# Tap sizes in PSUM, the causal block added per head, GpSimd's sums in turns, and memory values made with tokens on partitions

## The chip, the core and the metric

The kernel runs on one core of a Trainium2 chip: TensorE (PE), VectorE (DVE), ScalarE (ACT), GpSimd (POOL) and SyncE (SP, which here only issues transfers). The metric is the device time of one execution in microseconds (us).

## The reference, cut to what matters

Two transformer-like blocks over 512 tokens of width 1024, in float32. The first block mixes with four kinds of heads (a short convolution, a dilated attention, a forgetting attention, a pooling mixer), then attends to a memory of 256 tokens, then runs a convolutional feed-forward part. The second block is a long convolution (Hyena) with a filter made by a small network, then a gated feed-forward part. What the change touches:

```python
# forgetting attention, 4 heads, query block i of 128 tokens
s = einsum("bhqd,bhkd->bhqk", qi * scale, k) + ci[..., None] - c[:, :, None, :]
s = where(kpos[None, :] <= t[:, None], s, NEG_INF);  p = softmax(s);  out = p @ v
# memory attention
k, v = split(memn @ w_kv, 2)          # 256 tokens x 1024, 4 heads of 256
# filter of the long convolution: taps, and their size per channel
h = (h @ w_out).reshape(L, 2, D) * exp(-t[:, :, None] * abs(decay))
g = concatenate([h[:, 0], 0, flip(h[1:, 1])]);  g = g / sum(abs(g), axis=0)
# gates of the forgetting attention: log_sigmoid(x_n @ w_gate + b), summed over tokens
```

## The kernel before, in words

The code writes out by hand what each engine does and in which order; engines run their own list in order and wait on named semaphores. The order within a list is therefore fixed, and a wait holds up all that stands behind it on that engine.

Weights come in pairs of 1 MB (`raw`, two buffers). ACT makes the high part of each pair (`w_hi`, L501), DVE the low part (`w_lo`, L931, signal `lo_ready`), and PE multiplies with three passes (high by high L1577, and the two mixed products L1578 and L1579), which stands in for a float32 product. A chunk is half a pair.

**The first 100 us**: `in_chunk(c)` makes the projections of the first block, 24 matmuls each. Between them PE runs small jobs in two spare banks: the norm's sum, the gates (64 matmuls with 4 output columns, L1714, and 4 with one, L1716), three layers of the filter's network (`mlp`, L1683), four rotations for the rotary embedding (`rotate`, L1689). DVE answers in a written order (`mlp_args`, `rope_cos`, `rope_sin_part`), ACT too.

**The unit loop**: `for u in range(32)`, one unit per head and query block; the heads with u of 16 or more are the forgetting attention. In each iteration PE makes the scores of unit u + 2 (`qk_unit`, L1766), one chunk of weights, the transposes of unit u - 1 (L1775) and the product with the values of unit u - 2 (L1785). DVE adds the bias and takes the minimum (`mask_unit`, L1128 and L1136, signal `masked`), normalises (L1142) and splits weights; ACT exponentiates (L618) and makes the bias (L628). With i = u - 16, iterations 16 to 31 carry two more jobs:

- `mem_chunk(i)`: chunks 0 to 7 make the memory's keys, 8 to 15 its values. Before, the values come out with features on partitions, DVE scales them into `v_stage` (L1246), PE transposes them (`mem_values`, L1842) into bank 2, and DVE copies them to `v_mem` (L1251).
- for every second i, `filter_taps(t)`, t = i/2: PE makes taps into banks 2 and 3 (L1823), DVE multiplies them by a decay that ACT made (L1214 and L650), ACT takes their sizes (`tap_sizes`, L673) into two tiles of SBUF, DVE adds those to `acc` (L1226, signal `size_sum`). POOL forms sums and differences of the taps (`gen`, L430 and L431) and folds them (L437); after the last fold it issues two small loads (L441) that ACT copies into the matrix `g_fwd` (L731, signal `g_patched`).

Behind the loop PE sums the sizes (`filter_size`, L1832), transforms the filter in eight steps (`filter_spectrum`, L1908), and goes on to `w_out` and the rest of the kernel, which the change leaves as it is.

Of the kernel before, what the change touches and what calls it, by code (L numbers as in the profile page):

```python
# [18 lines left out]
ALU = mybir.AluOpType  # L19
# [59 lines left out]
JOBS = ["norm", "gates", "mlp0", "norm_mem", "mlp1", "rot0", "rot1", "rot2", "rot3", "mlp2", "vt0", "vt1", "c_tok", "c_row",  # L79
# [17 lines left out]
def program(nc, a):  # L97
    with ExitStack() as ctx:
# [5 lines left out]
        def sem(name):  # L104
# [31 lines left out]
        rstd_tok = at("rstd_tok", [P, 4], F32, o); o += 32  # L136
        log_f = at("log_f", [P, 4, 4], F32, o); o += 64
# [47 lines left out]
        v_stage = at("v_stage", [P, 2, M], F32, 12 * KB)  # L185
# [5 lines left out]
        c_keys = [at("c_keys0", [P, T], F32, c2 + 6 * KB), at("c_keys1", [P, T], F32, 14 * KB)]  # L191
        bias = at("bias", [P, T], F32, c2 + 8 * KB)
# [6 lines left out]
        size_taps = [at("size_taps0", [P, T], F32, 58 * KB), at("size_taps1", [P, T], F32, 74 * KB)]  # L199
# [30 lines left out]
        tri_in, pool_in, late_in, mask_in, diag_in, x_again = (sem(n) for n in (  # L230
            "tri_in", "pool_in", "late_in", "mask_in", "diag_in", "x_again"))
# [23 lines left out]
        vt_done, vt_read = sem("vt_done"), sem("vt_read")  # L255
# [57 lines left out]


# [57 lines left out]
        def _(pool):  # L372
# [24 lines left out]
            def load_filter(half):  # L397

                cols = slice(half * T, (half + 1) * T)
                for rows in (slice(0, 64), slice(64, P)):  # L400
                    pool.dma_start(f_out[rows], a["f_out"][:, :, cols]).then_inc(late_in, 16)
                pool.dma_start(decay[:], a["decay"][:, :, cols]).then_inc(late_in, 16)

# [8 lines left out]
            load_filter(0)  # L412

            for t in range(8):
                half, n, w = t // 4, t // 2 % 2, t % 2
                eo = eo_gen[half]
                if t in (2, 4):

                    pool.wait_ge(biased, 2 * t)
                    load_keys(1 + t // 2)  # L420
                if t == 3:

                    pool.wait_ge(gen_exp, 8)
                    pool.wait_ge(gen_done, 4)
                    load_filter(1)
                pool.wait_ge(gen_taps, 2 * t + 2)
                if w == 0 and t:
                    pool.wait_ge(gen_fold, 2 * t)
# [3 lines left out]
                if w:  # L432
                    pool.wait_ge(gen_sum, 2 * t + 2)
                    pool.wait_ge(tap_size, 2 * t + 2)
                    z, d, x, y = (gen[:, i, :] for i in range(4))
                    for kind, one, other, op in ((0, z, x, ALU.add), (1, d, y, ALU.subtract), (2, d, y, ALU.add), (3, z, x, ALU.subtract)):
                        nc.gpsimd.tensor_tensor(eo[:, 2 * kind + n, :], one, other, op).then_inc(gen_fold, 1)  # L437
# [11 lines left out]
            pool.wait_ge(vt_done, 4)  # L449
# [40 lines left out]
        def _(act):  # L490
# [94 lines left out]
            root(1, M)  # L585
# [6 lines left out]
            A.activation(gate_tmp[:, 2, :], gate_tmp[:, 1, :], ACT.Ln, bias=1.0).then_inc(gate_log, 1)  # L592
            v_copy(5)
            mlp_layer(1)
            raw_copy(2)
            raw_copy(3)
# [24 lines left out]
            def bias_unit(u):  # L621

                s, i = UNITS[u]
                if i == 0:
                    act.wait_ge(c_keys_in[s % 2], 16 * ((s - 4) // 2 + 1))
                if u > 16:
                    act.wait_ge(masked, u)
                A.activation(bias[:, 0:(i + 1) * P], c_keys[s % 2][:, 0:(i + 1) * P], ACT.Identity,  # L628
                             bias=c_neg[:, i, s - 4:s - 3]).then_inc(biased, 1)
# [13 lines left out]
            def decays(t):  # L643

                half, n, w = t // 4, t // 2 % 2, t % 2
                act.wait_ge(decay_abs, half + 1)
# [6 lines left out]
            def keep_token0(half):  # L653

                act.wait_ge(token0_done, half + 1)
                if half:
                    act.wait_ge(biased, 12)
                    act.wait_ge(size_sum, 16)
                else:
                    act.wait_ge(masked, 16)  # L660
                A.copy(g_token0[half][:], ps[:, 3, :]).then_inc(token0_kept, 1)
                A.activation(size_taps[0][0:1, :], ps[0:1, 3, :], ACT.Abs).then_inc(token0_kept, 1)

            def tap_sizes(t):

                half, n, w = t // 4, t // 2 % 2, t % 2
                if t:
                    act.wait_ge(size_sum, 2 * t)
                else:
                    act.wait_ge(token0_size, 1)  # L670
                for d in range(2):
                    act.wait_ge(gen_taps, 2 * t + d + 1)
                    A.activation(size_taps[d][:], eo_gen[half][:, 4 * w + 2 * d + n, :], ACT.Abs).then_inc(tap_size, 1)  # L673

            exp_unit(0)
            for u in range(32):
# [36 lines left out]
                if i >= 0 and i % 2 == 1:  # L713
                    tap_sizes(i // 2)
                if i == 14:
                    act.wait_ge(qk_done, 32)
                    for q in range(2):
                        src = a["weights"][G_DRAM + q].rearrange("p (j r n c) -> p j r n c", j=2, r=2, n=4)
                        dst = g_fwd[:, q * CHUNK:(q + 1) * CHUNK].rearrange("p (j r n c) -> p j r n c", j=2, r=2, n=2)
                        for r in range(2):  # L720
                            act.dma_start(dst[:, :, r], src[:, :, r, 0:2, :]).then_inc(g_fwd_in, 16)
            keep_token0(1)
            copy_transposed(31, T)
            act.wait_ge(token0_size, 2)
            out_tile(5)
# [3 lines left out]
            for q in range(2):  # L729
                rows = g_fwd[0:1, q * CHUNK:(q + 1) * CHUNK].rearrange("p (j r n c) -> p j r n c", j=2, r=2, n=2)  # L730
                A.copy(rows[:, :, q, 0, :], mid_row_g[:, 2 * q:2 * q + 2, :]).then_inc(g_patched, 1)  # L731
                if q:
                    for j in range(2):
                        A.activation(rows[:, j, 0, 0, :], ones[0:1, :], ACT.Copy, scale=0.0).then_inc(g_patched, 1)
            split_pair(19)
# [188 lines left out]
        def _(dve):  # L924
# [134 lines left out]
            V.tensor_scalar(mean[:, 0:M], bank[:, 0:M], 1.0 / D, EPS, ALU.mult, ALU.add).then_inc(norm_mean, 1)  # L1059
            dve.wait_ge(norm_mean, 2)  # L1060
            V.engine_nop().then_inc(read, 1)
            dve.wait_ge(norm_root, 2)
            V.reciprocal(rstd_mem[:], mean[:, 0:M]).then_inc(norm_rstd, 1)
# [28 lines left out]
            rope_cos(1)  # L1092
            split_pair(4)
# [3 lines left out]
            rope_sin_part(0)  # L1097
            rope_sin_part(1)
# [1153 lines left out]
```

## Time and profile before

| what | us |
|---|---|
| median of three executions | 1525.85 (1521.45 to 1526.17) |
| the profiled execution, device time | 1526.68 |
| its span in the profile | 1524.8 |
| PE busy | 1459.8 (96%) |
| DVE busy | 883.6 (58%) |
| ACT busy | 552.8 (36%) |
| POOL busy | 120.1 (8%) |

In rows of the profile, a row of the timeline is: start, duration, engine, line, operation, output <- inputs, shapes, count, and in brackets the idle time just before it with what ended it. "PEclk" is the granted clock of TensorE as a share of 2.4 GHz; 0.50 is 1.2 GHz.

### The profile page before, as it was taken

Reading aid. Unit: us, or ns where it says so; the run is one execution under the profiler, and the core shown is the slowest. Engines: PE = TensorE matmul, PEld = TensorE weight load, DVE = VectorE, ACT = ScalarE, POOL = GpSimd, SP = SyncE. Lnnn points to the kernel's source line nnn. Section 1 sums busy time; section 2 is a strip of 40 time slices with the busy share of each in tenths; the row PEclk is TensorE's granted clock in tenths of the full one; section 3 lists DMA queues with packets and bytes.
Section 4 is the critical chain, followed back from the end, with each engine's and each line's share of the span. In section 5 each row is a group of like instructions: output and inputs, shape, how many; then the busy total and the mean of one; then the engine's idle time right before and its main releaser. Section 6 shows DMA issues by size and latency. Waiting matters only on the chain.

```text
span 1524.8 us, 17410 instructions
## 1 busy us (share of the span) xinstructions
PE 1459.8 (96%) x6492; PEld 1163.5 (76%) x6492; DVE 883.6 (58%) x1152; ACT 552.8 (36%) x736; POOL 120.1 (8%) x134
## 2 busy tenths in 40 slices
PE   7899998889998999999999999999999999999995
PEld 6776667646886888888888878886788888888884
DVE  6745588633543577547736687675775433443446
ACT  5424355322333354324323454441233322221231
POOL 1000043420000000000000022103100000000000
PEclk9799997889998999999999999999999999999998
DMA  6211222332220223232323233223122222222221
GB/s 243 75 56 56 97 91 90 109 140 83 83 83 29 83 83 110 84 110 83 110 83 111 83 111 110 83 97 138 42 87 107 86 99 96 105 88 106 90 104 56
DMA packets 25501, 144.01 MB, mean 94 GB/s; under 512 B 3058, under 2 KB 6283, under 8 KB 10720
## 3 DMA queue, kind: packets, MB, share of 16 engines
q1 hardware_dynamic: 20464, 127.93, 23.8%
q0 software_dynamic: 3168, 11.87, 2.2%
q10 hardware_dynamic: 1808, 3.35, 0.6%
q8 instruction: 43, 0.70, 0.2%
q14 instruction: 18, 0.15, 0.0%
HBM read 136.84 MB, written 6.30 MB: 94 GB/s over the span
## 4 chain that ended last, share of the span: by engine, by line
PE 88%; DVE 6%; ACT 3%; issue 2%; DMA 1%; POOL 0%; DVEq 0%; SPq 0%; ACTq 0%; POOLq 0%
PE ps L1577 26%; PE ps L1579 25%; PE ps L1578 25%; PE ps L1908 2%; ACT w_hi L501 1%; DVE w_lo L931 1%; DVE acc L1226 1%; PE ps L1963 1%; PE ps L1785 1%; PE ps L1766 1%; PE ps L1950 1%; PE ps L1714 1%; PE ps L1823 1%; PE ps L2073 1%; PE ps L1775 1%
## 5 line engine op out<-in xcount | busy, mean ns | idle before, releaser
L1577 PE MATMUL ps<-opA_hi,w_hi 128*128 128x512 f32 x1120 | 445.8, 398 | 10.1 <-DVE opA_lo L976 9.5
L1579 PE MATMUL ps<-opA_hi,w_lo 128*128 128x512 f32 x1120 | 438.6, 392 | 0.0
L1578 PE MATMUL ps<-opA_lo,w_hi 128*128 128x512 f32 x1120 | 438.5, 392 | 0.0
L931 DVE TENSOR_TENSOR w_lo<-raw,w_hi 128x2048 fp32r<-128x2048 f32 x114 | 263.9, 2315 | 125.9 <-ACT w_hi L501 124.0
L501 ACT CAST w_hi<-raw 128x2048 fp32r<-128x2048 f32 x113 | 215.4, 1907 | 328.7 <-PE ps L1579 328.6
L1577 PEld LDWEIGHTS ps<-opA_hi,w_hi 128*128 128x128 f32 x1120 | 212.0, 189 | 63.6 <-issue 19.3
L1578 PEld LDWEIGHTS ps<-opA_lo,w_hi 128*128 128x128 f32 x1120 | 211.9, 189 | 45.1 <-issue 1.7
L1579 PEld LDWEIGHTS ps<-opA_hi,w_lo 128*128 128x128 f32 x1120 | 211.7, 189 | 45.0
L1577 PE MATMUL ps<-opB_hi,w_hi 128*128 128x512 f32 x576 | 227.6, 395 | 7.1 <-DVE spec L1502 2.8
L1579 PE MATMUL ps<-opB_hi,w_lo 128*128 128x512 f32 x576 | 225.8, 392 | 0.0
L1578 PE MATMUL ps<-opB_lo,w_hi 128*128 128x512 f32 x576 | 225.7, 392 | 0.0
L1577 PEld LDWEIGHTS ps<-opB_hi,w_hi 128*128 128x128 f32 x576 | 109.0, 189 | 35.1 <-issue 8.1
L1579 PEld LDWEIGHTS ps<-opB_hi,w_lo 128*128 128x128 f32 x576 | 109.0, 189 | 22.9
L1578 PEld LDWEIGHTS ps<-opB_lo,w_hi 128*128 128x128 f32 x576 | 109.1, 189 | 22.3
L1548 DVE TENSOR_TENSOR z_pad<-ps,rstd 128x512 f32<-128x512 f32 x44 | 30.1, 687 | 79.1 <-PE ps L1579 78.9
L1426 DVE TENSOR_TENSOR h<-ps,h 128x512 f32 x32 | 22.1, 691 | 81.5 <-PE ps L1579 81.5
L1403 DVE SCALAR_TENSOR_TENSOR conv<-z_pad,vecs,conv 128x512 f32<-128x512 f32 x88 | 64.0, 748 | 6.4 <-DVE conv L1403 0.5
L811 ACT CAST opB_hi<-conv 128x512 f32 x44 | 27.3, 620 | 107.6 <-DVE conv L1552 67.3
L967 DVE TENSOR_TENSOR opB_lo<-conv,opB_hi 128x512 f32 x44 | 30.5, 693 | 40.1 <-ACT opB_hi L811 40.1
L1336 DVE TENSOR_TENSOR h<-ps,h 128x512 f32<-128x512 f32 x32 | 22.1, 691 | 43.4 <-PE ps L1579 42.7
L753 ACT ACTIVATE opA_hi<-h,vecs 128x512 fp32r<-128x512 f32 x24 | 17.3, 723 | 76.5 <-DVE h L1336 51.9
L463 POOL TENSOR_TENSOR acc_next<-acc_next,sq_next 128x512 f32<-128x512 f32 x8 | 11.2, 1399 | 407.0 <-ACT sq_next L758 407.0
(326 smaller groups left out, 1544.8 us busy)
## 6 DMA issues: line engine op xcount, KB each, us to landing
raw<-weights_dram SPq DMA_DIRECT2D x113, 1024.0 KB, 4.8
g_dram<-g_stage POOLq DMA_DIRECT2D x8, 512.0 KB, 2.9
h<-x_t_dram SPq DMA_DIRECT2D x4, 512.0 KB, 8.1
h<-x_t_dram POOLq DMA_DIRECT2D x1, 2048.0 KB, 8.4
scores<-g_dram SPq DMA_DIRECT2D x4, 512.0 KB, 4.1
g_spec<-g_dram SPq DMA_DIRECT2D x4, 512.0 KB, 3.3
out_dram<-h ACTq DMA_DIRECT2D x4, 512.0 KB, 2.7
raw<-weights_dram SPq DMA_DIRECT2D x2, 512.0 KB, 6.6
```

What stands on the lines that cost most here:

```text
L501: A.copy(w_hi[:, p, :], raw[:, p, :]).then_inc(hi_ready, 1)
L811: A.copy(op_hi[1][:, bass.ds(2 * i + p, 1), :].rearrange("p a t -> p (a t)"), conv[:, p, 0, :] if not gated_only else conv[:, p, 1, :]).th ...
L931: V.tensor_tensor(w_lo[:, p, :], raw[:, p, :], w_hi[:, p, :].bitcast(F32), ALU.subtract).then_inc(lo_ready, 1)
L967: return V.tensor_tensor(out, src, hi.bitcast(F32), ALU.subtract)
L1336: V.tensor_tensor(h[:, k, :], ps[:, c % 4, :], h[:, k, :], ALU.add).then_inc(bank_read, 1)
L1403: ins = V.scalar_tensor_tensor(conv[:, p, j, :], z_pad[:, p, j, tap:tap + T], vecs[:, bass.ds(2 * i + (VEC["ffconv"] + tap * 2 * FT + j * ...
L1426: V.tensor_tensor(hd, ps[:, 2 * p + j, :], hd, ALU.add).then_inc(bank_read, 1)
L1548: V.tensor_tensor(z_pad[:, p, j, 0:T], ps[:, 2 * p + j, :], rstd[:], ALU.mult).then_inc(bank_read, 1)
L1577: W.matmul(out, w[0], x[0], start=start, stop=False, skip_group_check=mixed)
L1578: W.matmul(out, w[0], x[1], start=False, stop=False, skip_group_check=mixed)
L1579: return W.matmul(out, w[1], x[0], start=False, stop=stop, skip_group_check=mixed)
L1908: last = W.matmul(ps[:, bank + r, :], g_fwd[:, at_w:at_w + P], eo_gen[half][:, 2 * kind + k, :], start=(k == 0), stop=(k == 1))
```

## The change

Nine edits, all before 355 us of the profiled execution:

1. **Tap sizes in PSUM**: ACT writes them over the raw taps in banks 2 and 3, DVE adds them from there, in the same (odd) iteration; PE's next taps wait for that sum (`size_sum`) instead of for the product.
2. **Causal block per head**: POOL adds the 128 x 128 causal block to all four diagonal blocks of a head's keys at once (`diagonal_keys`); ACT makes the diagonal part of a unit's bias from it, in an instruction of its own. DVE's addition is gone.
3. **POOL in turns**: the sums of tap t start only when the split with `lo_ready` 13 + t is done, and half of each fold moves to the next turn.
4. **Memory values with tokens on partitions**: in chunks 8 to 15 the memory is the stationary operand and both halves of a weight pair move, 128 tokens by 256 features; DVE scales by a value per partition into `v_mem`. The transposes, `v_stage` and the copies are gone; `norm_mem` makes two columns more.
5. The absolute value of `decay` goes from DVE to ACT; the second load of `f_out` and `decay` goes from POOL's queue to ACT's, after `tap_sizes(3)`.
6. `filter_size(1)` comes after the second spectrum step, in bank 6; `token0_product(1)` uses bank 4.
7. ACT patches `g_fwd` before `out_tile(5)`.
8. `w_out` may start when seven of eight spectrum steps are read.
9. In the first stage the gates' four groups stand between quarters of `in_chunk(3)`, and `mlp(1)` behind `in_chunk(6)`, with the rotations ahead of it on PE, DVE and ACT.

```diff
+            def diagonal_keys(head):
+                pool.wait_ge(c_keys_in[head % 2], 16 * (head // 2 + 1))
+                nc.gpsimd.tensor_tensor(c_diag[head % 2][:].rearrange("p (i t) -> p i t", i=NT),
+                                        c_keys[head % 2][:].rearrange("p (i t) -> p i t", i=NT),
+                                        diag[:].unsqueeze(1).to_broadcast([P, NT, P]), ALU.add).then_inc(c_diag_made[head % 2], 1)
...
             for t in range(8):
-                if t in (2, 4):
-                    pool.wait_ge(biased, 2 * t)
-                    load_keys(1 + t // 2)
-                if t == 3:
-                    pool.wait_ge(gen_exp, 8)
-                    pool.wait_ge(gen_done, 4)
-                    load_filter(1)
+                if t < 7:
+                    pool.wait_ge(lo_ready, 13 + t)
+                if t in (0, 2):
+                    pool.wait_ge(biased, 4 + 2 * t)
+                    load_keys(2 + t // 2)
+                if w == 0 and t:
+                    fold(t - 1, (2, 3))
+                    pool.wait_ge(gen_fold, 2 * t)
                 pool.wait_ge(gen_taps, 2 * t + 2)
...
                 if w:
                     pool.wait_ge(gen_sum, 2 * t + 2)
                     pool.wait_ge(tap_size, 2 * t + 2)
+                    fold(t, (0, 1))
+                if t in (1, 3):
+                    diagonal_keys(2 + t // 2)
+            fold(7, (2, 3))
...
             def tap_sizes(t):
-                if t:
-                    act.wait_ge(size_sum, 2 * t)
                 for d in range(2):
                     act.wait_ge(gen_taps, 2 * t + d + 1)
-                    A.activation(size_taps[d][:], eo_gen[half][:, 4 * w + 2 * d + n, :], ACT.Abs).then_inc(tap_size, 1)
+                    A.activation(ps[:, 2 + d, :], eo_gen[half][:, 4 * w + 2 * d + n, :], ACT.Abs).then_inc(tap_size, 1)
...
+                if i == 7:
+                    act.wait_ge(gen_done, 4)
+                    act.wait_ge(gen_exp, 8)
+                    load_filter(act, 1)
...
-                    V.tensor_tensor(acc[:], acc[:], size_taps[d][:], ALU.add).then_inc(size_sum, 1)
+                    V.tensor_tensor(acc[:], acc[:], ps[:, 2 + d, :], ALU.add).then_inc(size_sum, 1)
...
-                V.tensor_tensor(dst, ps[:, i % 2, 0:M], rstd_mem[:], ALU.mult).then_inc(m_read, 1)
+                if i < 8:
+                    V.tensor_tensor(k_mem[:, i, :], ps[:, i % 2, 0:M], rstd_mem[:], ALU.mult).then_inc(m_read, 1)
+                else:
+                    hd, b = (i - 8) // 2, i % 2
+                    V.tensor_scalar(v_mem[:, b, hd * M:(hd + 1) * M], ps[:, b, 0:M], rstd_mem_tok[:, b:b + 1], None,
+                                    ALU.mult).then_inc(m_read, 1)
...
-                if i >= 2 and i % 2 == 0:
-                    add_sizes(i // 2 - 1)
+                if i >= 0 and i % 2 == 1:
+                    add_sizes(i // 2)
...
             def filter_taps(t):
-                    pe.wait_ge(gen_taps, 2 * t)
+                    pe.wait_ge(size_sum, 2 * t)
                 if t == 4:
-                    pe.wait_ge(late_in, 96)
-                if t >= 5:
-                    pe.wait_ge(vt_read, t - 4)
+                    pe.wait_ge(late_in[1], 48)
```

What moves is shown as the engines' lists have it; numbers behind a name tell buffers of one name apart.

PE, in the first stage: `in_chunk(3)` (L1577 to L1579 before), then the gates. Before:

```order
L1579 MATMUL ps<-opA_hi,w_lo 128x512
L1714 MATMUL ps<-gate_w,h 128x4 [waits gate_folded]
L1714 MATMUL ps<-gate_w,h 128x4 x7
L1716 MATMUL ps<-ones,acc 128x1
L1714 MATMUL ps<-gate_w,h 128x4 x8
L1716 MATMUL ps<-ones,acc 128x1
```

and of the change:

```order
L1729 MATMUL ps<-gate_w,h 128x4 x7
L1731 MATMUL ps<-ones,acc 128x1
L1591 MATMUL ps<-opA_hi,w_hi 128x512
L1592 MATMUL ps<-opA_lo,w_hi 128x512
L1593 MATMUL ps<-opA_hi,w_lo 128x512
L1591 MATMUL ps<-opA_hi,w_hi 128x512
L1592 MATMUL ps<-opA_lo,w_hi 128x512
L1593 MATMUL ps<-opA_hi,w_lo 128x512
L1729 MATMUL ps<-gate_w,h 128x4 x8
```

Six full matmuls now stand between two groups of small ones.

POOL, the sums and folds of taps 1 and 2 (L430, L431 and L437 before). Before:

```order
L430 TENSOR_TENSOR gen<-eo_gen_132 128x512 [waits gen_taps]
L431 TENSOR_TENSOR gen<-eo_gen_132 128x512
L437 TENSOR_TENSOR eo_gen_132<-gen 128x512 [waits tap_size,gen_sum]
L437 TENSOR_TENSOR eo_gen_132<-gen 128x512 x3
L395 DMA c_keys_126<-c_dram 128x512 [waits biased]
L430 TENSOR_TENSOR gen<-eo_gen_132 128x512 [waits gen_fold,gen_taps]
L431 TENSOR_TENSOR gen<-eo_gen_132 128x512
```

and of the change:

```order
L450 TENSOR_TENSOR gen<-eo_gen_134 128x512 [waits gen_taps,lo_ready]
L451 TENSOR_TENSOR gen<-eo_gen_134 128x512
L433 TENSOR_TENSOR eo_gen_134<-gen 128x512 [waits tap_size,gen_sum]
L433 TENSOR_TENSOR eo_gen_134<-gen 128x512
L419 TENSOR_TENSOR c_diag_128<-c_keys_126,diag 128x512 [waits c_keys_in0]
L404 DMA c_keys_127<-c_dram 128x512 [waits biased,lo_ready]
L433 TENSOR_TENSOR eo_gen_134<-gen 128x512 x2
L450 TENSOR_TENSOR gen<-eo_gen_134 128x512 [waits gen_taps,gen_fold]
L451 TENSOR_TENSOR gen<-eo_gen_134 128x512
```

Each turn now holds at most five operations and waits for a weight split; two folds of four come a turn later, and the causal block is new.

ACT, around the second load of the filter's matrix and decay, in iterations 23 and 24 of the change (before, POOL issued them and DVE took the absolute value):

```order
L697 ACTIVATE ps<-eo_gen_134 128x512 [waits gen_taps] x2
L321 DMA f_out<-f_out_dram 64x2x512 [waits gen_exp,gen_done]
L321 DMA f_out<-f_out_dram 64x2x512
L322 DMA decay<-decay_dram 128x2x512
L522 CAST w_hi<-raw 128x2048 [waits chunk_done,raw_in1]
L639 ACTIVATE scores,total<-scores,low 128x256 [waits masked]
L651 ACTIVATE bias<-c_keys_126,c_neg 128x256 [waits masked]
L652 ACTIVATE bias<-c_diag_128,c_neg 128x128
L660 COPY probs_t<-ps 128x512 [waits pv_done,transposed]
L672 ACTIVATE decay<-decay 128x1024 [waits late_in1]
L677 ACTIVATE eo_gen_135<-decay,vecs 128x512 [waits decay_abs]
```

The loads are issued one iteration ahead of the instruction that waits for them.

## Rows read from the trace of the kernel before

**Rows 1.** The page: TensorE's clock in 40 slices of the span.

```profile
PEclk9799997889998999999999999999999999999998
```

**Rows 2.** Stretches: busy time and count of each engine, clock, DMA share, GB/s.

```profile
38.40:52.10 13.70, 13.70 (x55) 11.96 (x55) 11.36 (x24) 5.05 (x8) 2.12 (x4) 0.50 0.37 130
60.30:72.50 12.20, 8.34 (x22) 4.84 (x21) 9.38 (x17) 8.82 (x12) 0.00 (x0) 0.72 0.25 86
197.47:221.00 23.53, 22.57 (x146) 17.20 (x144) 19.98 (x35) 14.67 (x28) 10.54 (x7) 1.00 0.18 64
221.00:300.76 79.76, 66.12 (x371) 53.00 (x370) 60.88 (x94) 34.71 (x65) 33.44 (x25) 0.85 0.31 97
300.76:319.32 18.56, 12.67 (x64) 10.48 (x64) 10.62 (x13) 5.33 (x12) 10.70 (x9) 0.70 0.32 107
```

**Rows 3.** PE's waits, 196 to 320 us: total, times, longest.

```profile
PE ps L1766 <- DVE low L1136: 7.0, 4, 2.8
PE ps L1823 <- DVE v_mem L1251: 4.6, 2, 2.4
PE ps L1832 <- DVE acc L1219: 3.5, 1, 3.5
PE ps L1908 <- DVE filter_norm L1237: 2.4, 1, 2.4
PE ps L1832 <- DVE acc L1226: 1.9, 1, 1.9
```

**Rows 4.** DVE's groups, 221.00 to 300.76 us: busy, mean ns, idle before.

```profile
L931 DVE TENSOR_TENSOR w_lo<-raw,w_hi 128x2048 fp32r<-128x2048 f32 x6 | 16.2, 2702 | 7.0 <-ACT w_hi L501 7.0
L1226 DVE TENSOR_TENSOR acc<-acc,size_taps 128x512 f32<-128x512 f32 x10 | 15.8, 1577 | 0.2
L1128 DVE TENSOR_TENSOR bias<-bias,diag 128x128 f32<-128x128 f32 x10 | 6.8, 685 | 1.4 <-ACT bias L628 1.2
L1214 DVE TENSOR_TENSOR eo_gen<-ps,eo_gen 128x512 f32<-128x512 f32 x10 | 6.4, 681 | 5.3 <-PE ps L1823 5.3
L1232 DVE SCALAR_TENSOR_TENSOR decay<-decay 128x1024 f32<-128x1024 f32 x1 | 2.3, 2302 | 1.6 <-DMA decay<-decay_dram 1.6
L1251 DVE COPY v_mem<-ps 128x512 f32<-128x512 f32 x3 | 2.0, 679 | 0.0
```

**Rows 5.** Timeline of DVE and POOL, 198 to 226 us.

```profile
198.87 0.28 DVE L1128 TENSOR_TENSOR bias<-bias,diag 128x128 f32<-128x128 f32 x1
206.19 2.29 DVE L931 TENSOR_TENSOR w_lo<-raw,w_hi 128x2048 fp32r<-128x2048 f32 x1 [0.36 <-ACT w_hi L501]
224.01 1.27 POOL L430 TENSOR_TENSOR gen<-eo_gen 128x512 f32<-128x512 f32 x1
```

**Rows 6.** Timeline of PE: chunks 1 and 5, and unit 22's scores.

```profile
198.42 0.39 PE L1577 MATMUL ps<-mg_hi,w_hi 128*128 128x256 f32 x1
213.96 0.91 PE L1766 MATMUL ps<-qk 64*128 64x384 f32 x2 [0.95 <-DVE low L1136]
221.00 0.39 PE L1577 MATMUL ps<-mg_hi,w_hi 128*128 128x256 f32 x1
```

**Rows 7.** The last taps and what follows, by engine.

```profile
300.86 1.29 DVE L1214 TENSOR_TENSOR eo_gen<-ps,eo_gen 128x512 f32<-128x512 f32 x2 [1.80 <-PE ps L1823]
307.42 5.82 POOL L437 TENSOR_TENSOR eo_gen<-gen 128x512 f32<-128x512 f32 x4 [1.84 <-ACT size_taps L673]
313.19 1.04 POOL L441 DMA_DIRECT2D mid_row_g<-weights_dram  x2
354.95 0.47 PE L1577 MATMUL ps<-opB_hi,w_hi 128*128 128x512 f32 x1 [1.01 <-DVEq L1322]
```

**Rows 8.** The tile `decay`, 150 to 360 us: its loads' time to landing.

```profile
DMA to landing us min/median/max: 4.9/6.0/7.0
```

**Rows 9.** First stage, PE: the third gates group, and a rotation.

```profile
38.78 3.55 PE L1714 MATMUL ps<-gate_w,h 128*128 128x4 f32 x16
66.91 2.07 PE L1689 MATMUL ps<-rope_raw,rot 128*128 128x512 f32 x2 [3.25 <-DVE mlp_x L1042]
```

More of the change, by code:

```diff
@@ L312, in end, with load_filter @@
                 self.origin, self.n = None, self.before + count * self.per
+        def load_filter(queue, half):
+            cols = slice(half * T, (half + 1) * T)
+            for rows in (slice(0, 64), slice(64, P)):
+                queue.dma_start(f_out[rows], a["f_out"][:, :, cols]).then_inc(late_in[half], 16)
+            queue.dma_start(decay[:], a["decay"][:, :, cols]).then_inc(late_in[half], 16)
         @block.sync
@@ L411, in _, with fold @@
             pool.wait_ge(sc_mul, 2)
-            load_filter(0)
+            load_filter(pool, 0)
+            def diagonal_keys(head):
[3 more added lines that the diff above has]
+                                        diag[:].unsqueeze(1).to_broadcast([P, NT, P]), ALU.add).then_inc(c_diag_made[head % 2], 1)
+            pool.wait_ge(diag_in, 16)
+            diagonal_keys(0)
+            diagonal_keys(1)
+            def fold(t, kinds):
+                half, n = t // 4, t // 2 % 2
+                z, d, x, y = (gen[:, i, :] for i in range(4))
+                for kind in kinds:
+                    one, other, op = ((z, x, ALU.add), (d, y, ALU.subtract), (d, y, ALU.add), (z, x, ALU.subtract))[kind]
+                    nc.gpsimd.tensor_tensor(eo_gen[half][:, 2 * kind + n, :], one, other, op).then_inc(gen_fold, 1)
             for t in range(8):
@@ L645, in decays @@
                 half, n, w = t // 4, t // 2 % 2, t % 2
+                if t % 4 == 0:
+                    act.wait_ge(late_in[half], 48)
+                    A.activation(decay[:], decay[:], ACT.Abs).then_inc(decay_abs, 1)
                 act.wait_ge(decay_abs, half + 1)
@@ L734, in _ @@
                         A.activation(rows[:, j, 0, 0, :], ones[0:1, :], ACT.Copy, scale=0.0).then_inc(g_patched, 1)
+            act.wait_ge(biased, 16)
+            out_tile(5)
             split_pair(19)
@@ L1058, in _ @@
             bank, read = job_bank("norm_mem")
-            V.tensor_scalar(mean[:, 0:M], bank[:, 0:M], 1.0 / D, EPS, ALU.mult, ALU.add).then_inc(norm_mean, 1)
+            V.tensor_scalar(mean[:, 0:M + 2], bank[:, 0:M + 2], 1.0 / D, EPS, ALU.mult, ALU.add).then_inc(norm_mean, 1)
             dve.wait_ge(norm_mean, 2)
@@ L1721, in _ @@
             pe.wait_ge(mem_sum, 5)
-            W.matmul(out[:, 0:M], ones[:], acc[:, 0:M], start=True, stop=True).then_inc(misc_done, 1)
+            W.matmul(out[:, 0:M], ones[:], acc[:, 0:M], start=True, stop=True)
+            for b in range(2):
+                last = W.matmul(out[:, M + b:M + b + 1], acc[:, b * P:(b + 1) * P], ones[:, 0:1], start=True, stop=True)
+            last.then_inc(misc_done, 1)
             in_chunk(5)
-            mlp(1)
             rotate(0)
@@ L1727, in _ @@
             in_chunk(6)
+            mlp(1)
             rotate(2)
             rotate(3)
+            in_chunk(7)
             mlp(2)
-            in_chunk(7)
             transpose_v(0, 0)
```

138 lines of the change are left out of this document (58 added, 80 removed).

## The prediction, made before the changed kernel ran

> **What bounds the kernel now.** I read the page first: TensorE's clock stands at 9 tenths or more in most of the 40 slices and dips in two places, slices 2 and 3 and slices 7 to 9 (38 us each) [rows 1]. Behind 355 us the clock is full to the end and the change touches nothing there, so whatever it is worth lies in the first 355 us. Next the stretches [rows 2]. Each shows which of two things costs PE its time: busy short of the stretch means PE waits, a clock under 1.00 means that it works at 1.2 GHz for a part. From 38.40 to 52.10 PE is busy throughout at clock 0.50. From 60.30 to 72.50 it is busy for 8.34 of 12.20 us at 0.72. From 197.47 to 221.00 all is well: 22.57 of 23.53 us at 1.00. From 221.00 to 300.76 it is busy for 66.12 of 79.76 us at 0.85, and from 300.76 to 319.32 for 12.67 of 18.56 at 0.70.
>
> The waits name the causes in the unit loop [rows 3]: 7.0 us for `masked` (DVE late with a unit's bias and minimum), 4.6 us for the copy of the memory values out of bank 2, 1.9, 3.5 and 2.4 us for the sums of tap sizes and what follows. All but one end on DVE, which is busy for only 60.88 of 79.76 us, but in a written order. Its groups say why [rows 4]. The addition of tap sizes, 128 x 512, takes 1577 ns, while the product of the same shape that reads one operand from PSUM takes 681. The 128 x 128 addition of the causal block takes 0.28 us alone [rows 5] and 685 ns in the mean here. A weight split takes 2.29 us alone [rows 5] and 2702 ns here. Those three read both operands from SBUF and slow down while POOL works (a POOL operation takes 1.27 us [rows 5]); the product beside them does not.
>
> **The unit loop: the main term.** What PE needs without waits is read from chunks 1 and 5: 221.00 - 198.42 = 22.58 us, less the one wait of 0.95, is 21.63 for four units, 5.41 each [rows 6]. From chunk 5 to chunk 15 are ten units, 54.1 us, and about 1 us more for the sum of sizes inside it. Against 79.76 [rows 2] that leaves 24.7, and with the wait of 0.95 ahead of it 25.6 us to be had if nothing else binds.
>
> Does DVE fit into 55 us? Taken from its 60.9: the size additions become one-operand-from-PSUM, 15.8 - 10 x 0.68 = 9.0; the block additions 6.8; the splits' excess 16.2 - 6 x 2.29 = 2.5; the absolute value 2.3; the copies of values 2.0 [rows 4, 5]. That leaves 38.3 of 55. ACT has 34.7 [rows 2]; a second bias instruction in three of four units and the absolute value (2.3 us on DVE, which I keep as the bound) bring it to some 41. POOL has 33.4 us of work, less what it spends blocked; a turn is four or five operations of 1.27 us, 5 to 6.4 us, and a period of two units is 10.8, so a turn that starts behind one split is over before the next. The values' chunks keep their 24 matmuls of 256 columns, so PE pays nothing for them and loses the transposes.
>
> The new wait: PE's taps now wait for `size_sum`. Behind it on PE stand the next unit's scores and chunk. The chain is ACT's copy, two absolute values and two additions, at some 0.7 us each (nearest row: 681 ns) and partly side by side, about 2.5 us behind the transposes of the odd unit; PE has one unit, about 5 us, before it asks. Cost nothing; if that cover were gone, a late sum would cost its lateness seven times.
>
> The load on ACT's queue is what I charge. `load_filter(act, 1)` stands behind `tap_sizes(3)`, about 1.5 us behind the transposes of unit 22, and PE asks for it 5 us behind those. Three issues and a landing of 4.9 to 7.0 us [rows 8] make it 1 to 4.5 us late. I take 2.8, plus 1 us for the clock, since the waits of 2.3 to 2.8 us before were each followed by a stretch at 1.2 GHz. Zero to 7.5 are the bounds. What is late next is ACT's own absolute value and decays, and DVE's product behind them, some 2 us, inside DVE's reserve.
>
> Unit loop: 25.6 - 3.8 = 21.8 us (18 to 25.6).
>
> **The end of the loop.** From chunk 15 to the first spectrum step were 18.56 us [rows 2]. DVE's last product ends at 302.15, POOL's folds at 313.24, its two loads are issued by 314.23 [rows 7]. In the change PE no longer waits for the sum of sizes, but for POOL's queue. Measured from chunk 15: the last split is done some 1.4 us ahead of it; turn 6 (two folds, two sums) ends at 3.7, the sums of tap 7 at 6.2, four folds at 11.3. From the last fold to a patched matrix there were at most 6.1 us before, with `out_tile` and PE's own waits in it; I take 3.6. So PE starts at 14.9 instead of 18.56: 3.7 us (1 to 5). PE sits idle for some 7 of them.
>
> **Spectrum and `w_out`.** `filter_size(1)` adds about 1.0 between two steps. `w_out` no longer waits 1.01 us [rows 7]. Together nothing.
>
> **The first stage.** The stretch at 1.2 GHz from 38.40 lasts 13.70 us, in which half the speed is lost: 6.9 us [rows 2]. It begins in the gates' groups, whose third takes 3.55 us [rows 9], and PE was never idle ahead of it. The stretch from 60.30 holds 3.86 us of waiting (3.25 of them ahead of a rotation, for DVE's read of `mlp(1)`'s bank [rows 9]) and, with the clock at 1.2 GHz for 6.8 us of which some 1.2 are idle, 2.8 us of lost speed. The new order puts both rotations and `in_chunk(6)` ahead of `mlp(1)`, so that wait has a chunk's cover: 3.9 + 2.8 = 6.7 us. The interleaved gates are the open cost: nothing, if the clock falls once as before; up to 6.9 more if it holds, of which PE gives some 3 back, since DVE's chain to `norm_mem` and `rope_cos(0)` keeps its length; 3 us less if the clock falls earlier and stays down through all four groups. I take "falls once", 6.7 (3.5 to 10.6), since between small groups of 1.8 us (half of 3.55, which is at 1.2 GHz) only six full matmuls stand.
>
> The Trainium skill speaks to it in "TensorE: Matmul & The Clock Gate", section "What's actually happening": the slow clock is the default and activity releases it. By that rule more full work inside the stretch is all to the good; this trace agrees so far that PE was busy with 4-column matmuls when the clock fell, not idle. It would make 1490 of the sum below.
>
> **Sum.** 21.8 + 3.7 + 0 + 6.7 = 32.2 us off the profiled 1526.7 (span 1524.8, about 1.9 around it), which stands 0.8 above the median: 1494.5, and I say 1494.
>
> **Rivals.**
> - *Clock holds through the gates* (0.2): 3.9 more, 1490. For it: six full matmuls between groups. Against: six of them take less time than the small group beside them.
> - *DVE or ACT binds the loop* (0.15): the order of `mask_unit`, split, taps and sizes leaves an idle engine and a late `masked`. If each period of two units takes 12.3 instead of 10.8 us, 7 us of the gain go, and the slow clock after each wait costs as much again: 1508. For it: ACT's idle time today all ends on DVE. Against: 38 of 55 us.
> - *POOL still collides* (0.1): the turns only set the earliest start, and `normalise` falls into them. Ten of them behind a POOL operation of 1.27 us would add 12.7 us to DVE's 38.3; that fills 51 of 55 and costs some 5 us: 1500. Against: the splits, the largest, stand outside the turns. The Trainium skill, "SBUF — State Buffer", section "SBUF: two separate sides", has it that DVE and GpSimd take one shared port pair in turns, each for a whole instruction, and that instructions in a two-port mode count too, not only those with two SBUF inputs. The rows agree with it for two inputs (0.28 against 685 ns).
> - *Slower than before* (0.04): PE waits for `size_sum` in every period. It decides from a chain of 10 us behind the transposes instead of 2.5: seven waits of 5 us are 35, more than all the gains, 1530. Nothing in the rows asks for it.
> - *No change* (0.03): the end of the loop eats the rest, because POOL's chain, now tied to the splits, ends 28 us later than I put it. It would need POOL operations of over 4 us.
>
> **Chances.** My forecast with its own range of 1488 to 1501 has 0.48. The range that leaves out no more than 2 in 10 adds the clock that holds, POOL's collisions and part of the loop's rival: 1484 to 1509. A difference of under 0.3% (4.6 us) can't be told from none in this kernel. Faster 0.93, the same 0.03, slower 0.04.
>
> **What would show it.** In the changed profile: DVE's size additions near 0.69 us; PE's waits for `masked` and `v_mem` gone, one wait of 1 to 4.5 us ahead of the fifth taps; ten units in about 58 us; PE idle for 6 to 8 us ahead of the first spectrum step, released by ACT's patch; a stretch at 1.2 GHz still beginning between 35 and 42 us; no wait of 3 us at the rotations. The prediction is wrong if the taps wait for `size_sum`, or if the scores still wait for DVE.

## The result, and the profile after

The changed kernel takes 1487.45 us in the median of four runs (1486.48 to 1490.03) against 1524.91 of the kernel before: a ratio of 0.9762, 95% interval 0.9737 to 0.9786. I had said 1494, with a range of 1484 to 1509. The profiled execution has a span of 1485.3 us, 39.5 less than the 1524.8 before; the sum in the prediction was 32.2. So 7.3 us more than in my sum are to be found.

The page's row of TensorE's clock, to be read beside [rows 1]:

```profile
PEclk9999999899999999999999999999999999999998
```

The first dip of before, which I had left where it was, is gone; of the second one slice is left, from 260 to 297 us, around the wait ahead of the first spectrum step. The stretches of the changed kernel, with the columns of [rows 2]: the gates' four groups with the quarters between them, chunks 1 to 5, chunks 5 to 15, chunk 15 to the first spectrum step, the spectrum to the first matmul of `w_out`:

```profile
30.54:42.78 12.24, 12.24 (x93) 11.46 (x93) 11.52 (x17) 1.98 (x2) 0.00 (x0) 1.00 0.18 75
187.25:208.79 21.54, 21.54 (x143) 17.00 (x142) 17.89 (x33) 15.73 (x31) 4.87 (x5) 1.00 0.20 68
208.79:267.07 58.28, 55.65 (x358) 44.17 (x357) 40.72 (x78) 37.81 (x73) 27.69 (x23) 0.97 0.33 115
267.07:283.12 16.05, 7.46 (x53) 5.86 (x52) 5.33 (x8) 4.26 (x11) 13.79 (x13) 0.81 0.47 143
283.12:317.23 34.11, 34.11 (x81) 14.09 (x81) 9.03 (x12) 6.26 (x9) 3.75 (x7) 0.94 0.45 182
```

Where the 39.5 us came from is read by the start of the same matmul in both traces. The first matmul of `c_tok` moved from 90.38 to 79.31 (11.1 us; I had said 6.7), and chunk 1 keeps that distance within 0.1. Chunks 1 to 15 give 1.0 and 21.5 (79.76 to 58.28), together 22.5 (said: 21.8). From chunk 15 to the spectrum 18.56 became 16.05: 2.5 (said: 3.7). The spectrum up to `w_out` gives 1.5 (said: 0), and everything behind it another 1.8 (said: 0): 11.1 + 0.1 + 22.5 + 2.5 + 1.5 + 1.8 = 39.5. Against the sum's terms that is 4.4 + 0.1 + 0.7 - 1.2 + 1.5 + 1.8 = 7.3: the first stage is where I was wrong.

PE's waits in the first 330 us, longest first, to be read beside [rows 3]. The first stands at the kernel's start and is there in both traces:

```profile
PE ps L1591 <- DVE opA_lo L1004: 9.6, 1, 9.6
PE ps L1922 <- issue: 8.6, 1, 8.6
PE ps L1828 <- DVE filter_norm L1259: 1.6, 1, 1.6
PE ps L1850 <- DMA decay<-decay_dram: 1.1, 1, 1.1
```

And DVE's groups in chunks 5 to 15, beside [rows 4]:

```profile
L959 DVE TENSOR_TENSOR w_lo<-raw,w_hi 128x2048 fp32r<-128x2048 f32 x5 | 11.4, 2289 | 0.8 <-ACT w_hi L522 0.8
L1252 DVE TENSOR_TENSOR acc<-acc,ps 128x512 f32<-128x512 f32 x10 | 6.9, 687 | 2.9 <-ACT ps L697 2.7
```

The size addition takes 687 ns instead of 1577, the split 2289 instead of 2702, and DVE is busy for 40.72 of 58.28 us. Of all the waits for DVE in the ten units one is left: 1.6 us for `filter_norm`, which I had overlooked. PE's one long wait now stands ahead of the first spectrum step, where the trace names no releaser ("issue"). The timelines of POOL, ACT and PE around it name one:

```profile
266.39 2.53 POOL L433 TENSOR_TENSOR eo_gen<-gen 128x512 f32<-128x512 f32 x2 [5.57 <-DVE w_lo L959]
269.00 1.35 POOL L450 TENSOR_TENSOR gen<-eo_gen 128x512 f32<-128x512 f32 x1
...
274.12 5.37 POOL L433 TENSOR_TENSOR eo_gen<-gen 128x512 f32<-128x512 f32 x4
279.44 1.03 POOL L462 DMA_DIRECT2D mid_row_g<-weights_dram  x2
...
281.90 0.71 ACT L757 COPY g_fwd<-mid_row_g 1x256 f32<-1x256 f32 x2 [7.56 <-DMA mid_row_g<-weights_dram]
...
283.12 5.74 PE L1922 MATMUL ps<-eo_gen,g_fwd 128*128 128x512 f32 x8 [8.59 <-issue]
```

The last turn waits for a split (5.57 us), POOL works its queue off, then issues two loads of 1 KB, and ACT sits idle for 7.56 us until they land.

### The profile page after: what moved, and what is told of

Its sections match the earlier page's. It is cut to its first block, busy times and chain, and to the rows that moved or that the text cites. A ratio compares the mean times of both kernels' runs of the same rounds, so it can differ in the third digit from the quotient of the medians.

```text
span 1485.3 us, 17372 instructions
## 1 busy us (share of the span) xinstructions
PE 1432.9 (96%) x6480; PEld 1143.4 (77%) x6480; DVE 856.3 (58%) x1131; ACT 558.7 (38%) x750; POOL 115.5 (8%) x135
## 4 chain that ended last, share of the span: by engine, by line
PE 91%; DVE 5%; ACT 2%; issue 1%; DMA 1%; ACTq 0%; DVEq 0%; SPq 0%
PE ps L1591 26%; PE ps L1593 25%; PE ps L1592 25%; PE ps L1922 2%; PE ps L1803 1%; PE ps L1784 1%; PE ps L1978 1%; PE ps L1850 1%; DVE w_lo L959 1%; PE ps L1965 1%; PE ps L1793 1%; ACT w_hi L522 1%; PE ps L1828 1%; PE ps L2088 1%; PE ps L1829 0%
```

## Experiments

Eleven kernels ran. Ratios are to the kernel before in the same set of runs. Its median was 1524.91 us in the changed kernel's set and 1524.65, 1522.96 and 1522.37 in those of the experiments, and its single executions lie up to 10.3 us apart. So medians of different sets that differ by 2 or 3 us say nothing by themselves, and I go by the start of the same matmul in the traces, of which there is one for each kernel. "Up to `w_out`" is the part that the change touches; what lies behind it is taken up at the end. Edits 5 to 8 were not run alone. None of these kernels leaves out or changes any part of what is computed.

**1. The two small loads ahead of the folds.**

```diff
+                if t == 4:
+                    pool.wait_ge(s_read, 4)
+                    (the two loads of mid_row_g)
...
             fold(7, (2, 3))
-            pool.wait_ge(s_read, 4)
-            (the two loads of mid_row_g)
```

> The changed kernel with one move: GpSimd issues its two small loads of mid_row_g at the start of turn 4 instead of behind the last fold. Theory (the idle time of 8.59 us ahead of the first spectrum step is the place of these two loads in GpSimd's queue, and nothing else): the first four steps read only the first half of the folds, which were done near 246 us, so TensorE starts once ScalarE has patched g_fwd, near 276 us of the profile instead of 283.12, with 1.5 us idle; the loop's stretch at 1.2 GHz of 10.24 us (5.1 us of lost speed) shrinks or goes. Sum: 7 to 12 us under the changed kernel, 1476 to 1480 us. Rival (the folds themselves bind, as my prediction reckoned when it counted them one by one): the wait only moves to the fifth step, which needs the last fold, or to the store of the first step's result, which is queued on GpSimd behind the folds; then 0 to 3 us, 1484 to 1487.

Measured: 1477.38 us (1475.38 to 1480.58), ratio 0.9705 (0.9667 to 0.9743), 10 us under the changed kernel. Its timeline, ACT and PE, and then the stretch from chunk 15 to the first step:

```profile
275.45 0.71 ACT L758 COPY g_fwd<-mid_row_g 1x256 f32<-1x256 f32 x2 [1.12 <-DMA g_fwd<-weights_dram]
...
276.67 3.67 PE L1923 MATMUL ps<-eo_gen,g_fwd 128*128 128x512 f32 x8 [2.15 <-issue]
```

```profile
267.06:276.67 9.61, 7.46 (x52) 5.86 (x52) 5.34 (x8) 4.26 (x11) 9.45 (x8) 1.00 0.61 201
```

6.4 us less to the first step. The clock now stays at 2.4 GHz there and through the spectrum behind it, where the changed kernel had 0.81 and 0.94; that gives two more by `w_out` (308.72 against 317.23: 8.5 in all). The rival is out: the folds themselves still end at 279.5, and no step waits for them. What bound the end of the loop was the place of two 1 KB loads in POOL's queue.

**2 to 4. The first stage.** The gates together again in the changed kernel; `mlp(1)` first again in the changed kernel; and the gates apart as the only edit of the kernel before.

```diff
 e2, and the reverse of it in e4:
-            for i in range(NT):
-                in_chunk(3, range(2 * i, 2 * i + 2))
+            in_chunk(3)
+            for i in range(NT):
                 (the eight small matmuls of group i)
 e3:
+            mlp(1)
             rotate(0)
             rotate(1)
             in_chunk(6)
-            mlp(1)
             rotate(2)
             rotate(3)
+            mlp(2)
             in_chunk(7)
-            mlp(2)
```

> The changed kernel with the gates' four groups of small matmuls behind one another again, behind all of in_chunk(3). Theory (the six full matmuls between two groups are what keeps TensorE at 2.4 GHz from 31 to 43 us): a stretch at 1.2 GHz of 10 to 14 us comes back between 35 and 50 us, 5 to 7 us are lost, of which the chain on VectorE may hide a part: 1490 to 1494 us. Rival (the clock would have held anyway, since the order of the work around it changed too): no such stretch, 1487 us.

> The changed kernel with mlp(1) back ahead of the rotations, and the order of the before kernel on all three engines; the gates stay apart. Theory (the wait ahead of a rotation was the order's, as predicted): TensorE again waits 3 to 5 us ahead of a rotation and the clock falls behind it, 4 to 8 us: 1491 to 1495. Rival (the wait was due to TensorE's own late start behind the slow stretch): the wait is under 1 us and the time 1487 to 1488.

> The kernel before with one edit: the gates' groups between quarters of in_chunk(3). Theory (that edit alone holds the clock): no stretch at 1.2 GHz between 37 and 51 us, 6.8 us less for TensorE, of which it may give back up to 3 in longer waits ahead of the rotations: 1518 to 1522 us against 1525. Rival (the clock falls once as before, my forecast): 1525.

Measured: e2 1491.99 us (1488.17 to 1494.17), ratio 0.9795 (0.9756 to 0.9834). e3 1493.26 (1492.10 to 1495.87), 0.9811 (0.9774 to 0.9848). e4 1519.69 (1515.46 to 1524.60), 0.9979 (0.9959 to 0.9999). The gates of e2 on PE's timeline; a window of 13.70 us over its slow stretch; and e3's wait:

```profile
34.60 1.84 PE L1728 MATMUL ps<-gate_w,h 128*128 128x4 f32 x16
36.52 2.05 PE L1728 MATMUL ps<-gate_w,h 128*128 128x4 f32 x16
38.86 3.55 PE L1728 MATMUL ps<-gate_w,h 128*128 128x4 f32 x16
```

```profile
36.90:50.60 13.70, 13.70 (x63) 12.35 (x64) 11.48 (x20) 5.55 (x8) 2.13 (x4) 0.55 0.30 107
```

```profile
63.40 1.12 PE L1703 MATMUL ps<-rope_raw,rot 128*128 128x512 f32 x2 [3.26 <-DVE mlp_x L1070]
```

In the changed kernel all four groups take 1.84 us and the stretch that holds them has clock 1.00. Together again, the third takes 3.55 as before [rows 9], and TensorE runs at 1.2 GHz from 38.15 to 51.85 us (the window shown has the same length but starts 1.3 us ahead of that, so its mean is 0.55). The order of e3 also puts `mlp(2)` back ahead of `in_chunk(7)`. `c_tok` starts at 84.06 in e2 and at 85.77 in e3 against 79.31: the gates are worth 4.8 us there and the order of `mlp(1)` and `mlp(2)` 6.5, together the 11.1 measured within 0.2. In e4 it moves from 90.38 to 85.47, 4.9. The theories of e2 and e3 hold. That of e4 holds in the time, whose interval just excludes no change, and not in the clock: it named no stretch at 1.2 GHz between 37 and 51 us, and there is one of 3.4 us from 43.3 on, in the full matmuls behind the last group (0.63 us each, 0.39 or 0.40 at full clock):

```profile
40.78 1.84 PE L1714 MATMUL ps<-gate_w,h 128*128 128x4 f32 x16
...
44.37 0.63 PE L1579 MATMUL ps<-opA_hi,w_lo 128*128 128x512 f32 x1
...
46.85 0.40 PE L1579 MATMUL ps<-opA_hi,w_lo 128*128 128x512 f32 x1
```

e3, e1 and e9 have the same short stretch; the changed kernel, e5, e6, e7, e10 and e11 have none, though up to there the list of PE is the same in all of them but e4. So the gates apart are followed by 0 or 3.4 us at 1.2 GHz instead of 13.7. It is no cost at `c_tok` in e1 (79.28 against 79.31), where two waits of 0.5 and 0.6 us of the changed kernel are gone. Another stretch of 3.4 us stands behind `c_tok` in the kernel before, the changed kernel, e1, e3, e4, e7, e8 and e9 and is missing in the rest. It is missing in e2, and so the gates are worth only 3.1 us at chunk 1 (190.38 against 187.25); the order of e3 is still worth 6.6 there.

**5 and 6. Which cure did the unit loop need?** The block on VectorE; and with it the tap sizes in SBUF.

```diff
 e5:
-                    (diagonal_keys on POOL, two bias instructions on ACT)
+                    S.link(V.tensor_tensor(bias[:, i * P:n], bias[:, i * P:n], diag[:], ALU.add))
 e6, besides:
-                    A.activation(ps[:, 2 + d, :], eo_gen..., ACT.Abs)
+                    A.activation(size_taps[d][:], eo_gen..., ACT.Abs)
-                    V.tensor_tensor(acc[:], acc[:], ps[:, 2 + d, :], ALU.add)
+                    V.tensor_tensor(acc[:], acc[:], size_taps[d][:], ALU.add)
```

> The changed kernel with the causal block back on VectorE, one 128 x 128 addition for each unit's bias; GpSimd's copies of the keys are left out. Theory (VectorE has the room: 41.5 of the 59.2 us of the last ten units are busy): ten additions of 0.28 us alone to 0.69 us beside GpSimd are 3 to 7 us of its 17.7 us of idle time, and TensorE sees at most a new wait of 0.5 us: 1487 to 1489 us. Rival (what counts is the length of the chain from ScalarE's bias to the minimum that releases the scores, not VectorE's sum): TensorE waits again for the minimum in two or more units, each wait followed by a slow stretch: 1491 to 1496.

> The one before it, and the tap sizes back in SBUF as well (written there by ScalarE, added from there by VectorE, at the new place in the order). Theory (two operands in SBUF are what makes the addition slow beside GpSimd): its mean is 1.2 to 1.6 us instead of 0.71, 8 to 14 us more for VectorE, which then fills the ten units; scores and taps wait again: 1493 to 1505. Rival (GpSimd's turns have taken it out of the additions' way): the mean stays near 0.7 us and the time within 2 us of the one before it.

Measured: e5 1488.16 us (1486.42 to 1491.17), ratio 0.9768 (0.9733 to 0.9804); e6 1491.69 (1489.35 to 1495.37), 0.9803 (0.9765 to 0.9842). DVE's additions of sizes in e6:

```profile
L1239 DVE TENSOR_TENSOR acc<-acc,size_taps 128x512 f32<-128x512 f32 x10 | 7.5, 751 | 2.5 <-ACT size_taps L681 2.3
```

With two operands in SBUF they take 751 ns, not 1577: the mean is the one that the rival of e6 named. Its bound on the time, 2 us, is missed, as the medians stand 3.5 us apart; but the intervals overlap, and by the traces e6 reaches the first spectrum step at 285.68 and e5 at 285.69 and `w_out` at 320.70 and 320.56, so the loop does not notice. The block costs the loop more than its theory had: both kernels reach the first step 2.6 us later than the changed kernel, though they are 1.3 to 1.4 us ahead of it at chunk 1 (they lack the stretch at 1.2 GHz behind `c_tok`). They have one new wait of 0.8 us (e5) or 0.5 (e6) for the minimum, and 6.8 us at 1.2 GHz from 230 us on where the changed kernel has 3.4 at 239. In e5's median only 0.7 us of it shows. With the block on DVE the sizes' place in PSUM is worth nothing in the loop, as long as POOL keeps its turns.

**7. No turns.**

```diff
-                if t < 7:
-                    pool.wait_ge(lo_ready, 13 + t)
```

> The changed kernel without the turns: GpSimd's sums start as soon as their taps are there, whatever VectorE is doing; the half folds stay where they are. Theory (the sizes in PSUM and the room on VectorE have made the turns worthless, my rival of collisions was mispriced): the splits go from 2.29 to 2.7 us or more, TensorE waits no more than before in the ten units, and the last turn begins 3 to 5 us earlier, so that the first spectrum step does too: 1483 to 1487 us. Rival (the turns protect the splits, on which the chunks wait): 5 us and more lost in the loop, 1490 to 1497.

Measured: 1480.61 us (1479.81 to 1484.08), ratio 0.9730 (0.9692 to 0.9767), 7 us faster than with them and below the 1483 to 1487 of the theory. DVE's groups by form, first with turns (the changed kernel), then without; and one row of POOL's timeline without:

```profile
L1168 DVE TENSOR_SCALAR scores<-scores,inv_total 128x512 f32<-128x512 f32 x2 | 1.7, 829 | 0.1
L1168 DVE TENSOR_SCALAR scores<-scores,inv_total 128x128 f32<-128x128 f32 x2 | 0.6, 286 | 0.1
```

```profile
L956 DVE TENSOR_TENSOR w_lo<-raw,w_hi 128x2048 fp32r<-128x2048 f32 x5 | 14.4, 2878 | 0.2 <-ACT w_hi L519 0.2
L1165 DVE TENSOR_SCALAR scores<-scores,inv_total 128x512 f32<-128x512 f32 x3 | 4.2, 1408 | 0.1
L1165 DVE TENSOR_SCALAR scores<-scores,inv_total 128x128 f32<-128x128 f32 x2 | 2.6, 1277 | 0.1
```

```profile
216.94 3.34 POOL L448 TENSOR_TENSOR gen<-eo_gen 128x512 f32<-128x512 f32 x1
```

The collisions are there, and larger than I thought: 1277 for 286 ns. In its ten units DVE is busy for 47.88 of 57.66 us (40.72 of 58.28 with turns), and no wait of PE is longer than with turns. What the turns cost is mostly at the end, where POOL starts its last turn late: from chunk 15 to the first step are 13.91 us instead of 16.05. The first step stands at 280.15 instead of 283.12, `w_out` at 313.91 instead of 317.23. So 3.3 of the 7 us are the turns'; the other half lies behind `w_out`, where no edit reaches and where I can't lay it to them (see the end).

**8. The memory values alone, in the kernel before.** `mem_chunk`, `mem_tile` and `norm_mem` as in the changed kernel; the transposes, `v_stage` and the copies deleted; all else as before.

> The kernel before with one edit: memory values with tokens on partitions, no transposes, no staging, no copies. Theory (the waits of 4.6 us for the copy in bank 2 were the edit's to take, and the clock behind them): 4.6 us of waiting, four groups of four transposes (0.6 us each) and up to 3 us of the slow stretch go, 5 to 9 us in all: 1516 to 1520 against 1525. Rival (VectorE is late anyway, so the wait moves to the minimum or to the sum of sizes): 0 to 3 us.

Measured: 1515.58 us (1509.32 to 1519.09), ratio 0.9948 (0.9927 to 0.9969). Chunk 15 starts at 289.51 instead of 300.76, of which 0.6 was there at the first chunk. The waits for `masked` stay as they were (7.0 us in four); those for `v_mem` are gone, with new ones of 2.6 us for the normalised scores and 1.0 for ACT's copy of their transposes. So by its trace this edit alone brings 10.6 us in the loop, more than the 5 to 9 of the theory; the medians stand 7.4 us apart, inside them.

**9. Neither cure.** The kernel of e6, without the turns.

> The block on VectorE and the sizes in SBUF, as in the run with both, and GpSimd without its turns. Theory (turns and PSUM are two cures for one illness, and either alone would have done): the size additions rise from 0.75 to 1.3 us and more, the block's to 0.7 or more, with the slower splits and scalings (2.9 and 1.0 us) VectorE has over 58 us of work in 59, scores or taps wait for it and the clock falls behind the waits: 1495 to 1510 us. Rival (VectorE still keeps up, because what made it late before was the written order, not the load): within 3 us of the run without turns, 1478 to 1484.

Measured: 1495.16 us (1493.94 to 1495.67), ratio 0.9812 (0.9782 to 0.9841). Its size additions, and its new wait:

```profile
L1236 DVE TENSOR_TENSOR acc<-acc,size_taps 128x512 f32<-128x512 f32 x8 | 11.2, 1404 | 2.8 <-ACT size_taps L678 2.7
```

```profile
PE ps L1834 <- DVE acc L1236: 2.4, 1, 2.4
```

The theory holds in the time and in PE's wait; DVE is busy for 53.97 of the 65.04 us of its ten units, not for nearly all of them. Without turns, PSUM and the block off DVE are worth 14.5 us in the medians (1495.16 against 1480.61), of which 9.6 show at `w_out` (323.55 against 313.91) and 7.4 from chunk 1 to chunk 15; with turns, 4.2 in the medians (1491.69 against 1487.45) and 3.5 at `w_out`. With both in place, the turns are a loss of 3.3.

The loop's balance, from chunk 1 to chunk 15: 102.34 us before, 91.73 in e8, 79.82 in the changed kernel, 86.62 in e9, where the main parts of edits 1 to 3 are undone (the places in the order stay). So edit 4 by itself gives 10.6 and those parts of edits 1 to 3 give 6.8 with the others in place; the 5.1 that remain, edit 5 and what the edits give only together, no run tells apart.

**10 and 11. The three moves.**

```diff
+                if i == 7:
+                    (load_filter(act, 1) with its two waits, at the start of the iteration)
                 if u in SPLITS:
...
+                if i == 9:
+                    filter_size(0)
                 if u in (9, 17, 25):
                     (low part of out_tile)
```

> The changed kernel with three moves: mid_row_g loaded in turn 4; the second filter load issued at the start of iteration 23 instead of its end; the reciprocal of filter_size(0) ahead of the low part of out_tile on VectorE. Theory: beside the 10 us of the first move, the waits of 1.1 and 1.6 us in the loop go, and the slow stretch of 3.4 us behind the second (1.7 us of lost speed): 1472 to 1474 us. Rival (the order behind those waits makes the next one late): 1476 to 1478, as with the first move alone.

> The same without GpSimd's turns. Theory (the turns were worth something at the end of the loop only because the mid-row loads stood behind the last folds; with these moved nobody waits for the folds): the same as with turns within 2 us, 1471 to 1475 us, though VectorE's splits and scalings are slower. Rival one (the turns cost time of themselves, 7 us as in the run without them): 1465 to 1468. Rival two (with TensorE's waits gone the collisions on VectorE begin to show): 1477 and more.

Measured: e10 1476.25 us (1472.05 to 1476.99), ratio 0.9680 (0.9648 to 0.9713); e11 1475.24 (1473.52 to 1479.55), 0.9685 (0.9650 to 0.9719). Chunks 5 to 15 of e10:

```profile
207.44:261.49 54.05, 54.05 (x359) 42.66 (x358) 41.70 (x78) 37.67 (x73) 28.64 (x25) 1.00 0.38 123
```

PE is busy throughout at full clock: 54.05 us, which is the 54.1 that the prediction worked out for ten units without waits. From chunk 1 to chunk 15 e10 takes 4.2 us less than e1, so both waits and the slow stretch are gone, as the theory said; a new stretch of 3.4 us at 1.2 GHz at 271 us costs 1.7 of it again, and 1.4 us were there at chunk 1 already, where e10 and e11 lack the stretch behind `c_tok`. `w_out` starts at 304.61, 4.1 us ahead of e1; but the time falls by only 1.1, in the range that the rival named, since 2.9 of them are lost behind `w_out`. So the place is confirmed and the whole is not: neither of e10 and e11 can be told from e1. e11 starts `w_out` at 304.60: it loses 2.6 us in the loop and has them back by the end of the spectrum. With the loads moved, the turns are worth nothing either way, as the theory of e11 had it.

## Why the prediction came out as it did

- **The unit loop** was right in its main reasons: 22.5 against 21.8, DVE at 40.72 us against 38.3, ACT at 37.81 against 41. The load on ACT's queue was late by 1.1 us, at the lower edge of 1 to 4.5; its place in the balance was filled by the wait of 1.6 us for `filter_norm`, which I had not named, with 3.4 us at 1.2 GHz behind it. It comes from the same illness: the reciprocal stands on DVE behind `out_tile`'s low part, and this waits for ACT (in e10 it stands ahead, and the wait is gone). That the sum came so near is partly luck: I charged 3.8 us where 58.28 - 54.05 = 4.2 were lost, and took 55.1 us for ten units and the sum of sizes where 54.05 hold both.
- **The step that failed: "The interleaved gates are the open cost ... I take 'falls once'."** In the changed kernel's trace the clock does not fall; where it does fall with the gates apart (e1, e3, e4, e9), it is behind them and for 3.4 us. I argued that six full matmuls take less time than the small group beside them (1.5 us against 1.84), so that the mixture would look like the small groups. e2 and e4 show that it doesn't: 4.8 and 4.9 us at `c_tok`. That was the rival of 0.2, priced at 3.9. With it the first stage gave 11.1, above the 10.6 that bounded it; the total stayed in its range because that range had room for this rival. The rule of the Trainium skill that I weighed there ("TensorE: Matmul & The Clock Gate", section "What's actually happening": slow is the default, activity releases the clock) gave 1490 and stood nearer to the result than my reading of the row. The traces agree with it so far: in e2 the clock fell in small matmuls without a pause and came back 4 us into the full ones, and with full ones between the groups it held.
- **`mlp(1)` and the rotations**: 6.5 us in e3 against 6.7. By e3 the wait of 3.3 us ahead of the rotation comes back with the order, and 3.4 us at 1.2 GHz behind it.
- **The end of the loop**: 2.5 against 3.7; PE starts 16.05 us after chunk 15, not 14.9, and is idle for 8.6, not 7. The count of POOL's operations was right; the last turn started later than I put it.
- **Spectrum and `w_out`**: 1.5 against 0. The wait of 1.0 is gone and `filter_size(1)` takes 0.95, as reckoned. The slow clock took 2.9 us there before (mean 0.92 over 35.63 us) and 2.0 after (0.94 over 34.11), which I had not counted; the remaining half microsecond is not accounted for.
- **The taps' wait for `size_sum`** cost nothing, as said, until e9 took its cover away: 2.4 us.
- **The collision rival** (0.1, 1500 us) was wrong in sign for the end: the turns do their work on DVE, but DVE has the room without them. The Trainium skill, "SBUF — State Buffer", section "SBUF: two separate sides", names instructions in a two-port mode beside those with two SBUF inputs. The trace agrees so far that an instruction with one large input is held up too: e7's scaling of 128 x 128 takes 1277 ns with POOL at work, and 286 in the changed kernel while POOL is idle; whether it runs in such a mode no row shows. And one POOL addition takes 3.34 us beside a split.
- **Behind `w_out`** I had 0; the trace has 1.8. I had written that the clock is full behind 355 us, but [rows 1] has an 8 in its thirteenth slice, 457 to 496 us: 10.3 us there run at 1.2 GHz, and 6.8 more near 1055 us. The changed kernel has 3.5 us less of it.

## What to carry to other kernels

Once a loop is free of waits, look at what each queue still has to issue behind it: here two 1 KB loads behind the last folds cost 8.5 us up to `w_out`, nearly as much as the one edit of the loop that was run alone gives there (10.6). Cures for one illness do not add: price each with the others in place, and leave out the one (here the turns) that has a cost of its own. Small matmuls that have to run were cheaper here scattered among full ones; a stretch of them also slowed the full ones that followed.

## What the runs showed of the chip that I had not expected

- Four groups of sixteen matmuls of 4 columns, 1.84 us each, with six full matmuls (1.5 us) between them, ran at 2.4 GHz in every trace that has them apart, from the first group to the last. Back to back, with the same work in sum, they bring 13.7 us at 1.2 GHz (e2), the last 4 us of which lie in the full matmuls behind them. What comes behind the last separate group is not fixed by the order of work: with one list on PE up to there, three traces have 3.4 us at 1.2 GHz in the full matmuls (e1, e3, e9) and six have none.
- Behind `w_out` all kernels do the same work with the same waits within 0.8 us, and yet this part took 1169.85 us before, 1168.07 in the changed kernel, 1164.19 in e7, 1166.88 in e1 and 1169.79 in e10. PE's busy time differs with it. The stretches of before, e7 and e10:

```profile
354.95:1524.80 1169.85, 1140.38 (x5040) 933.22 (x5040) 662.71 (x774) 406.03 (x477) 50.31 (x63) 0.99 0.26 91
```

```profile
313.91:1478.10 1164.19, 1135.18 (x5042) 930.34 (x5040) 663.55 (x775) 406.84 (x478) 50.34 (x63) 0.99 0.26 91
```

```profile
304.61:1474.40 1169.79, 1140.71 (x5042) 933.62 (x5040) 663.39 (x775) 407.77 (x478) 50.27 (x63) 0.99 0.26 91
```

  The busy time of the same matmuls differs by 5.5 us, and that is the clock: leaving out the last 16 us, before and e10 run for 17.1 us at 1.2 GHz, the changed kernel for 13.6, e1 for 10.2 and e7 for 6.8, half of which is lost. These stretches lie at the same places in all five, some 110, 130 and 700 us behind the start of `w_out`, but some of them are short or missing in some traces. Which of them comes, and how long it is, I could not tell; this stays open. With one trace for each kernel the runs do not show either whether it belongs to the kernel or changes from execution to execution; the 10.3 us between executions of the kernel before leave room for the second. It means that a gain of 3 us in the first stages can be lost or doubled behind them, as in e10 and e7.
